# Sample attention as one straight pipeline of eight samples, and the causal mask of the recurrent heads put ahead of the gate scaling

## The chip, the core and the metric

One core of a Trainium2 chip runs the whole kernel. The metric is the time of one execution in microseconds (us) of device time. PE is TensorE, ACT ScalarE, DVE VectorE, POOL GpSimd, SP the engine that only issues transfers; a name with q (SPq, ACTq) is the instruction queue of that engine. All numbers are float32; a float32 matmul shows as two passes in the trace, a transpose as one.

## What is computed

One hybrid layer over a prompt of 512 tokens and 8 samples of 8 new tokens each. The parts that the change touches are the recurrent heads (the decay weights `exp(logd - m)` under a causal mask, and the normed, gated output) and the attention of each sample over 4096 cached positions. Cut to that:

```python
def mlstm_chunk(carry, inp):                     # 4 heads of 256
    logd = jnp.where(causal, b[..., :, None] - b[..., None, :] + li[..., None, :], -jnp.inf)
    s = jnp.einsum('bhtd,bhsd->bhts', q, k) * jnp.exp(logd - m_t[..., None])
    num = jnp.einsum('bhts,bhsv->bhtv', s, v) + a[..., None] * jnp.einsum('bhtd,bhdv->bhtv', q, C)
...
    h = h * jax.nn.sigmoid(o_pre)...
    h = rms_norm(h, norm_w).reshape(B, T, M_WIDTH)
    out = (h * jax.nn.silu(z.astype(jnp.float32))).astype(u.dtype)

def compress(rows, pe, w1, w2, k_norm):          # one vector per 16 positions, two layers
    hid = per[:, :-1, 0] + per[:, 1:, 1] + bias[:, None, :]
    out = jnp.einsum('bncgh,chd->bncgd', jax.nn.silu(hid), w2)
    return rms_norm(out[:, :, 0], k_norm), out[:, :, 1]

def nsa_sample(...):                             # for each of the 8 samples
    past = cache_kv[layer, page_table, :, 0:2]...          # 32 pages of 128 positions
    kc, vc = compress(...)
    o_cmp, idx = nsa_compressed(qq, tq, kc_b, vc_b, c_end, n_slc)   # top 16 of 65 blocks
    # o_sel: attention over the chosen blocks; o_win: over the last 512 positions
    o = gg[:, 0] * o_cmp + gg[:, 1] * o_sel + gg[:, 2] * o_win
    a_out = a_out * jax.nn.silu(az)
```

## The kernel before

The program runs stages one behind the other, each a block in which every engine has its own instruction list, in the order in which it is written, with semaphores between them: `project_in`, `mlstm_heads`, `compress_prompt`, `attend_prompt`, `attend_samples`, `combine_samples`, `project_out`. Nothing reorders an engine's list: an instruction that waits holds up all that stands behind it on its engine. At a block's end all engines meet.

**Recurrent heads.** For head h PE makes the scores of four 128-row tiles and of the samples (`scores`, L726 and L729) into two buffers `m_st`; ACT makes the decay weights `m_weights` (L846); POOL masks them (`causal`, L922), DVE multiplies scores and weights (L999) and so frees the score buffer for PE. POOL also scales the output gates by the norm weight (`norm_gate`, L915), for which it waits on transfers (the last is `landing<-m_norm_w`, issued by SP when the outputs of the head before are done). On POOL `norm_gate(h)` stands ahead of `causal(h)` for heads 1 to 3. DVE's `outputs(h)` waits for `norm_gate(h)`.

**Samples.** `attend_samples` sets up buffers and calls `sample_turn` nine times: once with compression alone (sample 0), six times in a hardware loop over b, and twice more. Each call is a block of its own with its own semaphores. A turn of the loop attends for sample b and compresses sample b+1:

- *pages.* A sample has 32 pages. Of each page one half (256 KB, `wide<-pages`, the buffer `comp`) feeds the compression and the other (256 KB, `s_kv<-pages`) the scores and values of the chosen blocks. `load_pages` looks up the page numbers of 8 pages in `ptab` (one register load each, L1457) and then issues the 8 transfers (L1460). SP loads three quarters of `s_kv` and all of `comp`; ACT loads the last quarter of `s_kv`, 8 pages, at the start of a turn.
- *compression.* PE: `hidden(i)`, four groups of 8 steps (L1529, one step is 128 weights by 512 columns) into two buffers `s_pH`; ACT splits each group out (L1648, L1649); POOL adds the two halves (L1808), ACT makes the sigmoid in three activations (L1654 to L1656), POOL multiplies (L1811); PE `second_layer` (L1541), ACT copies (L1665, L1668), POOL squares, sums and scales the keys (L1816 to L1826), PE turns them (L1550), ACT copies them to `s_kcT` (L1678).
- *attention.* Scores of the compressed keys (L1562) and the window (L1568), softmax by DVE and ACT, the turned probabilities and values, the choice of blocks on DVE (L1747 to L1757); then nine parts of scores over the cache (L1604, eight of 512 columns), which DVE masks (L1769) and of which it takes the maximum (L1776); ACT exponentials (L1714); and nine times: turn (L1619), copy on DVE (L1789), multiply with the values (L1629: all 128 query rows by 256 value columns, of which each row needs 64).
- the three results of a sample go to `o_scratch` in memory; `combine_samples` loads them all, applies the gates, adds and turns them and stores them for `project_out`.

Of the kernel before, what the change touches and what calls it, by code (L numbers as in the profile page):

```python
# [7 lines left out]
F32 = mybir.dt.float32  # L8
# [6 lines left out]
P = 128  # L15
# [547 lines left out]
def mlstm_heads(nc, B, a, o):  # L563
# [5 lines left out]
    with Semaphores(nc) as sem, ExitStack() as ctx:  # L569
# [329 lines left out]
        def _(pool):  # L899
# [502 lines left out]
def attend_samples(nc, B, a, o):  # L1402


    with ExitStack() as ctx:
        sb = lambda n, s, d=F32: ctx.enter_context(nc.sbuf_tensor(n, s, d))
        ps = lambda n, s: ctx.enter_context(nc.psum_tensor(n, s, F32))
        S = B.sample = Buffers()
        S.comp, S.kvp = B.comp, sb("s_kv", [P, NPG, CH])
        S.wnd = sb("s_wnd", [P, 2 * 2 * WIN])  # L1410
        S.cw1 = sb("cw1_sample", [P, 2, 8, P])
        S.scores = sb("s_scores", [P, PAST + TSA])
        S.first, S.second = sb("s_first", [P, KV * PAST // SEG]), sb("s_second", [P, KV * PAST // SEG])
        S.hidg = sb("s_hidg", [P, KV, NCMP_S + 1])
        S.kcn, S.kcms = sb("s_kcn", [P, 2, KV * AD]), sb("s_kcms", [P, 2 * KV])
        S.kcT, S.vc = sb("s_kcT", [P, 2, 256]), sb("s_vc", [P, 2, KV * AD])
        S.probT = sb("s_probT", [P, 2, 4, P])
        S.qb, S.nm = sb("s_qb", [P, 2, 64]), sb("s_newmask", [P, TSA])
        S.pgp, S.imp, S.top = sb("s_pgp", [32, 264]), sb("s_imp", [32, 72]), sb("s_top", [32, 2, 8])
        S.bias = sb("s_bias", [P, NBLK])  # L1420
        S.mx, S.rs, S.col = sb("s_mx", [P, 16]), sb("s_rs", [P, 16]), sb("s_col", [P, 8])
        S.rows = sb("s_rows", [P, 3, AD])
        S.pS, S.pT, S.pO, S.pH = (ps(n, [P, 2, CH]) for n in ("s_pS", "s_pT", "s_pO", "s_pH"))
        with Semaphores(nc) as sem, nc.Block() as block:
            loaded, zero = sem("s_loaded"), sem("s_zero")

            @block.sync
            def _(sp):
                sp.dma_start(S.cw1[:], a["cmp_w1"]).then_inc(loaded, 16)
                sp.wait_ge(loaded, 16)  # L1430

                sp.wait_ge(B.comp0_in, 16 * NPG)

            @block.vector
            def _(dve):
                nc.vector.memset(S.imp[:], 0.0)

                nc.vector.memset(S.kcn[:], 0.0)
# [7 lines left out]
        with nc.Fori(0, NB - 2) as b:  # L1446
            sample_turn(nc, B, a, b, attend=True, compress=True, load=True)
# [791 lines left out]
```

## Time and profile before

| | us |
|---|---|
| median of 3 runs | 2437.31 (2436.68 to 2440.33) |
| the profiled execution | 2436.53 |
| its span | 2434.8 |
| first hidden step of sample 0 to first transfer of `project_out`, in the trace | 1227.5 to 1954.0 |

The page of the profile gives busy time by engine, the span in 40 slices, the chain that ended last and the costliest groups. Busy time of PE counts the modelled length of each pass, so a stage can show PE at 90% and still lose time; a table of windows (busy time, granted clock and transfer share in stretches that one chooses) and the instructions in order of time show where.

### The profile page before, as it was taken

To read this page: it belongs to the slowest core of one execution; us is meant where nothing else is said; L and a number is where in the kernel's file an instruction comes from. 1 tells how busy PE (TensorE), PEld (TensorE's weight loads), DVE (VectorE), ACT (ScalarE), POOL (GpSimd) and SP (SyncE) were. 2 spreads that over 40 slices of the span, in tenths; PEclk is the share of its full clock that TensorE was granted. 3 is DMA by queue.
4 is the path that set the end of the run, shared out by engine and by line. 5 is a ranking of instruction groups with operands and counts; after the bars stand their busy time and mean duration, and the time that the engine had idled before them with its cause. 6 is when DMAs were issued, how large, how long until landed. Compare 5 with 4: busy or idle time off the path is not lost. (4 is left out here: it accounts for less than half of the span.)

```text
span 2434.8 us, 34702 instructions
## 1 busy us (share of the span) xinstructions
PE 2143.9 (88%) x12851; PEld 1740.2 (71%) x12851; DVE 851.7 (35%) x1644; ACT 697.7 (29%) x1337; POOL 154.1 (6%) x192
## 2 busy tenths in 40 slices
PE   7999999999988887799857889888986569999998
PEld 7999999999985555655533554455444369999998
DVE  6233255233323334456502233223323432233232
ACT  6332223333323222156511222122212031133221
POOL 0000000000001000000011121012111001010000
PEclk9999999999998887599978889988997779999999
DMA  5542333333313333111136657665753272222330
GB/s 188 172 152 75 93 98 112 98 107 98 113 65 125 129 132 121 47 53 57 61 125 233 218 191 241 226 226 186 240 198 114 63 283 94 70 90 76 98 103 25
DMA packets 167331, 316.19 MB, mean 130 GB/s; under 512 B 22365, under 2 KB 71902, under 8 KB 164130
## 3 DMA queue, kind: packets, MB, share of 16 engines
q1 hardware_dynamic: 156536, 297.33, 36.9%
q10 hardware_dynamic: 10666, 17.05, 2.1%
q8 instruction: 91, 1.49, 0.3%
q14 instruction: 38, 0.31, 0.0%
HBM read 281.53 MB, written 41.05 MB: 132 GB/s over the span
## 5 line engine op out<-in xcount | busy, mean ns | idle before, releaser
L250 PE MATMUL mm<-x_hi,w_hi 128*128 128x288 f32 x1696 | 369.1, 299 | 14.3 <-DVE w_lo L381 14.3
L250 PE MATMUL mm<-x_lo,w_hi 128*128 128x288 f32 x1696 | 364.1, 296 | 0.0
L250 PE MATMUL mm<-x_hi,w_lo 128*128 128x288 f32 x1696 | 364.1, 296 | 0.0
L250 PEld LDWEIGHTS mm<-x_hi,w_hi 128*128 128x128 f32 x1696 | 274.8, 190 | 15.9 <-issue 12.2
L250 PEld LDWEIGHTS mm<-x_lo,w_hi 128*128 128x128 f32 x1696 | 274.5, 190 | 0.0
L250 PEld LDWEIGHTS mm<-x_hi,w_lo 128*128 128x128 f32 x1696 | 274.2, 189 | 0.0
L381 DVE TENSOR_TENSOR w_lo<-w_raw,w_hi 128x1024 fp32r<-128x1024 f32 x106 | 129.8, 1225 | 386.4 <-ACT w_hi L280 386.4
L1529 PE MATMUL s_pH<-wide,cw_sample 128*128 128x512 f32 x512 | 239.4, 624 | 9.7 <-PEq L86 9.7
L1970 PE MATMUL o_mm<-o_feat_hi,o_w_hi 128*128 128x288 f32 x1024 | 225.7, 302 | 24.5 <-DVE o_feat_lo L2045 17.7
L1970 PE MATMUL o_mm<-o_feat_lo,o_w_hi 128*128 128x288 f32 x1024 | 222.0, 299 | 0.0
L1970 PE MATMUL o_mm<-o_feat_hi,o_w_lo 128*128 128x288 f32 x1024 | 221.6, 299 | 0.0
L280 ACT ACTIVATE w_hi<-w_raw 128x1024 fp32r<-128x1024 f32 x106 | 112.1, 1058 | 344.4 <-PE mm L250 344.4
L1529 PEld LDWEIGHTS s_pH<-wide,cw_sample 128*128 128x128 f32 x512 | 100.2, 201 | 130.1 <-issue 128.8
L1970 PEld LDWEIGHTS o_mm<-o_feat_hi,o_w_hi 128*128 128x128 f32 x1024 | 168.7, 192 | 26.9 <-issue 22.8
L1970 PEld LDWEIGHTS o_mm<-o_feat_lo,o_w_hi 128*128 128x128 f32 x1024 | 167.6, 192 | 0.0
L1970 PEld LDWEIGHTS o_mm<-o_feat_hi,o_w_lo 128*128 128x128 f32 x1024 | 167.5, 191 | 0.0
L1629 PE MATMUL s_pO<-s_kv,s_probT 128*128 128x256 f32 x512 | 134.2, 410 | 0.5 <-DVE s_probT L1789 0.5
L1629 PEld LDWEIGHTS s_pO<-s_kv,s_probT 128*128 128x128 f32 x512 | 100.8, 208 | 16.9 <-DVE s_probT L1789 3.1
L2039 DVE TENSOR_TENSOR o_w_lo<-o_w_raw,o_w_hi 128x2048 fp32r<-128x2048 f32 x32 | 73.4, 2293 | 111.4 <-ACT o_w_hi L2000 111.4
L1789 DVE COPY s_probT<-s_pT 128x512 f32<-128x512 f32 x64 | 44.1, 691 | 119.7 <-PE s_pT L1619 119.7
L1604 PE MATMUL s_pS<-s_kv,s_qb 128*64 128x512 f32 x256 | 68.9, 632 | 16.4 <-DMA s_kv<-pages 8.5
L2000 ACT ACTIVATE o_w_hi<-o_w_raw 128x2048 fp32r<-128x2048 f32 x32 | 60.8, 1900 | 49.2 <-DMA o_w_raw<-w_out 49.2
(395 smaller groups left out, 2487.6 us busy)
## 6 DMA issues: line engine op xcount, KB each, us to landing
wide<-pages SPq DMA_DIRECT2D x256, 256.0 KB, 4.1
w_raw<-w_in SPq DMA_DIRECT2D x106, 512.0 KB, 4.0
s_kv<-pages SPq DMA_DIRECT2D x192, 256.0 KB, 4.9
s_kv<-pages ACTq DMA_DIRECT2D x64, 256.0 KB, 7.3
o_w_raw<-w_out SPq DMA_DIRECT2D x16, 1024.0 KB, 7.8
o_w_raw<-ple_gate SPq DMA_DIRECT2D x16, 1024.0 KB, 6.7
m_state<-state SPq DMA_DIRECT2D x4, 2056.0 KB, 11.9
state_sample<-m_state SPq DMA_DIRECT2D x4, 2056.0 KB, 6.7
```

What stands on the lines that cost most here:

```text
L250: last = nc.tensor.matmul(mm[:, s % 3, y, 0:HALF], w[:, m % RING, kk, :], f[:, k, y * HALF:(y + 1) * HALF], start=k == 0 and i == 0, stop= ...
L280: s_.activation(whi[:, m % RING], raw[:, m % RING], ACT.Copy).then_inc(whi_done, 1)
L381: v.tensor_tensor(wlo[:, m % RING], raw[:, m % RING], whi[:, m % RING].bitcast(F32), ALU.subtract).then_inc(wlo_done, 1)
L1529: last = mm(S.pH[:, c, :], S.cw1[:, c, k, :], S.comp[:, 16 * cc:16 * cc + 16, k * 64 + c * 32:k * 64 + c * 32 + 32], start=k == 0, stop=k ...
L1604: last = mm(S.pS[64 * gp:64 * gp + 64, j % 2, :], S.qb[:, gp, :], S.kvp[:, 4 * j:4 * j + 4, gp * P:(gp + 1) * P], start=True, stop=True)
L1629: last = mm(S.pO[:, 0, 0:256], S.probT[:, q % 2, i, :], S.kvp[:, 4 * q + i, 256:512], start=q == 0 and i == 0, stop=False)
L1789: last = v.tensor_copy(S.probT[:, j % 2], S.pT[:, j % 2, :].rearrange("p (n r) -> p n r", r=P))
L1970: last = nc.tensor.matmul(mm[:, j % 2, x, 0:HALF], w[:, j % 2, k, :], f[:, k, cols], start=k == 0 and i == 0, stop=k == KD - 1 and i == 2)
L2000: s_.activation(whi[:, j % 2], raw[:, c % 2, :, (j % 2) * P:(j % 2 + 1) * P], ACT.Copy).then_inc(whi_done, 1)
L2039: v.tensor_tensor(wlo[:, j % 2], raw[:, (j // 2) % 2, :, (j % 2) * P:(j % 2 + 1) * P], whi[:, j % 2].bitcast(F32), ALU.subtract).then_inc( ...
```

## The change

**Heads.** POOL runs `causal(h)` ahead of `norm_gate(h)` for heads 1 to 3.

**Samples.** One function, one block, no loop and no `combine_samples`. All eight samples stand written out one behind the other on each engine, with semaphores that count on. The work of a sample stays the same in kind, with these differences:

- SP loads the window, all of `comp` and quarters 0 and 2 of `s_kv`; ACT loads quarters 1 and 3. The page numbers of a whole call (8 or 16) are looked up first, then the transfers are issued.
- `second_layer` (8 matmuls of 128 columns by a block-diagonal `s_cw2`, in place of 16 of 64 columns) and `keys_turned` of sample b moved from the end of the turn before to this turn's start, between the hidden groups of sample b+1.
- The values matmuls are done for two halves of the query rows, each with its own 128 value columns (64 weights by 128 columns, side by side in the array).
- DVE masks and takes the maximum in one instruction (`tensor_tensor_reduce`), and does the compression's sums and products that POOL did. POOL has nothing left in a turn.
- The gates are applied when a result is read out; three matmuls (`gather`) put a sample's output in place, and one transfer stores all at the end.

```diff
             for h in range(1, MH):
                 sample_u(h)
+                causal(h)
                 norm_gate(h)
-                causal(h)
...
+def load_pages(eng, ptab, pages, dst, part, first, begin, end, sem):
+    numbers = [eng.value_load(ptab[0:1, first + i:first + i + 1], min_val=0, max_val=pages.shape[0] - 1) for i in range(begin, end)]
+    for i, page in zip(range(begin, end), numbers):
+        eng.dma_start(dst[:, i, :], pages[bass.ds(page, 1), :, part * CH:(part + 1) * CH].rearrange("x p c -> p (x c)")).then_inc(sem, 16)
...
+            sp.dma_start(cw1[:], a["cmp_w1"]).then_inc(cw1_in, 16)
+            sp.dma_start(wnd[:], a["win_pages"][0]).then_inc(wnd_in, 16)
+            load_kv(sp, 0, 0)
...
+            sp.wait_ge(h_done, 2)
+            load_comp(sp, 1, 0, HP)
+            load_kv(sp, 0, 2)
+            sp.wait_ge(h_done, 4)
+            load_comp(sp, 1, HP, NPG)
+            for b in range(NB):
+                if b + 2 < NB:
+                    sp.wait_ge(h_done, 4 * (b + 1) + 2)
+                    load_comp(sp, b + 2, 0, HP)
+                if b + 1 < NB:
+                    sp.wait_ge(wo_done, b + 1)
+                    sp.dma_start(wnd[:], a["win_pages"][b + 1]).then_inc(wnd_in, 16)
+                if b + 2 < NB:
+                    sp.wait_ge(h_done, 4 * (b + 1) + 4)
+                    load_comp(sp, b + 2, HP, HP + QP)
+                if b + 1 < NB:
+                    sp.wait_ge(pv_done, PARTS * b + 2)
+                    load_kv(sp, b + 1, 0)
+                if b + 2 < NB:
+                    load_comp(sp, b + 2, HP + QP, NPG)
+                if b + 1 < NB:
+                    sp.wait_ge(pv_done, PARTS * b + 6)
+                    load_kv(sp, b + 1, 2)
...
+            for b in range(NB):
+                c = b + 1
+                window_scores(b)
+                hidden(c, 0, range(8))
+                if b:
+                    gather(b - 1)
+                second_layer(b)
+                hidden(c, 1, range(8))
+                keys_turned(b)
+                hidden(c, 2, range(0, 2))
+                compressed_scores(b)
+                hidden(c, 2, range(2, 5))
+                compressed_turned(b)
+                hidden(c, 2, range(5, 7))
+                compressed_values(b)
+                window_turned(b)
+                hidden(c, 2, range(7, 8))
+                hidden(c, 3, range(0, 2))
+                window_values(b)
+                block_bias(b)
+                for j in range(PARTS):
+                    scores(b, j)
+                    if j in (2, 4, 6):
+                        hidden(c, 3, range(1 + j // 2, 2 + j // 2))
+                hidden(c, 3, range(5, 8))
+                for j in range(PARTS + 1):
+                    if j < PARTS:
+                        turned(b, j)
+                    if j >= 1:
+                        values(b, j - 1)
...
+                act.wait_ge(wm_ready, b + 1)
+                s_.activation(pw[:, 0:WIN], pS[:, 1, :], ACT.Exp, bias=mx[:, 13:14], accum_out=rs[:, 13:14])
...
+                if b:
+                    act.wait_ge(pv_done, PARTS * b)
+                    load_kv(act, b, 3)
+                split(c, 0)
+                act.wait_ge(kv_done, b + 1)
...
+                act.wait_ge(mx_ready, b + 1)
+                for j in range(PARTS):
+                    if j == 2:
+                        split(c, 3)
+                    if j in (4, 5, 6):
+                        sigmoid(c, j - 4)
+                    s_.activation(chunk(j), chunk(j), ACT.Exp, bias=mx[:, 11:12], accum_out=rs[:, j:j + 1]).then_inc(p_ready, 1)
+                if c < NB:
+                    act.wait_ge(pv_done, PARTS * b + 4)
+                    load_kv(act, c, 1)
```

How the order moved, at the three places that the prediction speaks of. On ACT, from the last exponentials of a sample (L1714 before, L1742 after) to the copy of the next keys. Before, with the block's end behind the last row:

```order
L1714 ACTIVATE s_scores,s_rs<-s_scores,s_mx 128x512 x8
L1714 ACTIVATE s_scores,s_rs<-s_scores,s_mx 128x64
L1665 ACTIVATE s_vc<-s_pH 128x256
L1665 ACTIVATE s_vc<-s_pH 127x256
L1668 ACTIVATE s_kcn<-s_pH 128x256
L1668 ACTIVATE s_kcn<-s_pH 127x256
```

After, with the rows of 8 pages standing once where "..." is (a lookup, L1890, and a transfer, L1892, each eight times):

```order
L1742 ACTIVATE s_scores,s_rs<-s_scores,s_mx 128x64
L1890 TENSOR_LOAD ptab
...
L1892 DMA s_kv<-pages 128x512
L1704 ACTIVATE s_scores,s_rs<-s_pS,s_mx 128x512
L1705 ACTIVATE s_scores,s_rs<-s_pO,s_mx 128x64
L1890 TENSOR_LOAD ptab
...
L1892 DMA s_kv<-pages 128x512
L1680 ACTIVATE s_first<-s_pH 64x512
L1681 ACTIVATE s_second<-s_pH 64x512
L1716 ACTIVATE s_kcn<-s_pT 128x256
```

Two bursts of eight page loads now stand between a sample's last exponential and the copy of the next sample's keys; before, one burst stood at a turn's start and the copies followed the exponentials directly.

On PE, from the last values of a sample to the turned keys of the next. Before, across the block's end (the branch):

```order
L1631 MATMUL s_pO<-vsel_new,s_probT 128x256
L1550 MATMUL s_pH<-ident,s_kcn 128x128
L1550 MATMUL s_pH<-ident,s_kcn 128x127
L1550 MATMUL s_pH<-ident,s_kcn 128x128
L1550 MATMUL s_pH<-ident,s_kcn 128x127
L1478 UNCONDITIONAL_BRANCH
```

After:

```order
L1618 MATMUL s_pO<-vsel_new,s_probT 64x128 x2
L1532 MATMUL s_pS<-s_wnd,qblk 64x512 x2
L1534 MATMUL s_pO<-kwin_new,qblk 64x64 x2
L1504 MATMUL s_pH<-wide,cw_sample 128x512 x8
L1625 MATMUL s_pO<-s_pick,s_out 128x64 x3
L1515 MATMUL s_pT<-s_cw,s_hidg 128x128 x4
L1515 MATMUL s_pT<-s_cw,s_hidg 127x128 x4
L1504 MATMUL s_pH<-wide,cw_sample 128x512 x8
L1523 MATMUL s_pS<-ident,s_kcn 128x128
```

There is no branch, and two hidden groups (L1504) stand between the values and the turned keys (L1523), which wait for ACT and DVE.

On POOL, in the recurrent heads (the copy L908 brings in a head's sample inputs):

```order
 L908 COPY m_us<-upad 128x64 x2
+L922 AFFINE_SELECT m_weights<-m_weights 128x128 x4
 L915 TENSOR_TENSOR m_sgz<-m_sgz,landing 128x256 x4
 L915 TENSOR_TENSOR m_sgz<-m_sgz,landing 64x256
+L908 COPY m_us<-upad 128x64 x2
 L922 AFFINE_SELECT m_weights<-m_weights 128x128 x4
```

The four masks now come before the five multiplications that wait for transfers.

## Rows read from the trace of the kernel before

**Rows 1.** The page: busy time and its share of the span.
```profile
PE 2143.9 (88%) x12851; PEld 1740.2 (71%) x12851; DVE 851.7 (35%) x1644; ACT 697.7 (29%) x1337; POOL 154.1 (6%) x192
```

**Rows 2.** Windows: stretch, length, busy time by engine, clock, transfer share, GB/s.
```profile
1227.40:1290.20 62.80, 36.90 (x100) 19.58 (x100) 0.00 (x0) 10.29 (x18) 13.01 (x12) 0.74 0.39 134
1290.20:1864.70 574.50, 493.21 (x1904) 280.55 (x1904) 177.13 (x462) 135.79 (x329) 91.36 (x84) 0.92 0.61 204
1864.70:1931.80 67.10, 42.41 (x172) 26.12 (x172) 25.65 (x66) 9.11 (x29) 0.00 (x0) 0.76 0.41 142
1931.80:1954.00 22.20, 1.11 (x8) 0.93 (x8) 6.68 (x7) 0.00 (x0) 0.00 (x0) 0.56 0.30 63
```

**Rows 3.** Order of time at a turn's start: start, us, engine, line, what, idle before.
```profile
1455.52 1.12 PE L1562 MATMUL s_pS<-s_kcT,s_qb 128*64 128x255 f32 x4 [6.61 <-ACT s_qb L1688]
```

**Rows 4.** Recurrent heads: scores of head 1 (two rows) and head 3, and DVE's wait.
```profile
814.47 4.97 PE L726 MATMUL m_st<-m_qh,m_kh 128*128 128x512 f32 x8
825.06 2.93 PE L726 MATMUL m_st<-m_qh,m_kh 128*128 128x256 f32 x8 [5.63 <-DVE m_weights L999]
...
933.74 6.40 PE L726 MATMUL m_st<-m_qh,m_kh 128*128 128x512 f32 x16
...
DVE m_weights L999 <- POOL m_weights L922: 38.2, 2, 19.2
```

**Rows 5.** Order of time, PE at full clock; x counts passes.
```profile
1101.48 2.38 PE L1273 MATMUL a_pO<-a_pT,landing 128*64 128x512 f32 x16
1103.79 1.13 PE L1242 MATMUL a_pS<-ksel,landing 64*128 64x512 f32 x4
...
1311.24 7.03 PE L1529 MATMUL s_pH<-wide,cw_sample 128*128 128x512 f32 x16
...
1441.35 0.60 PE L1619 MATMUL s_pT<-ident,s_scores 128*128 128x128 f32 x4
1441.79 1.89 PE L1629 MATMUL s_pO<-s_kv,s_probT 128*128 128x256 f32 x8
...
1886.13 1.94 PE L1604 MATMUL s_pS<-s_kv,s_qb 128*64 128x512 f32 x8
```

**Rows 6.** Page loads: order of time, ACT's group, and SP's shortest, median, longest issue (ns).
```profile
1199.91 0.34 SPq L1223 DMA_DIRECT2D cat_scratch<-a_cat  x1
1202.91 2.11 SPq L1220 DMA_DIRECT2D wide<-pages  x4
...
1295.57 4.63 ACTq L1460 DMA_DIRECT2D s_kv<-pages  x8
...
L1692 ACT ACTIVATE s_scores<-s_pS,s_mx 128x255 f32<-128x255 f32 x8 | 3.8, 472 | 79.4 <-issue 79.4
...
L1460 SPq DMA_DIRECT2D s_kv<-pages x192: 332/333/1441, 1296.0 to 1893.2; - x192
```

**Rows 7.** Groups of the samples' stage: busy us, mean ns of one, idle before.
```profile
L1714 ACT ACTIVATE s_scores<-s_scores,s_mx 128x512 f32<-128x512 f32 x64 | 45.2, 708 | 61.2 <-DVE s_mx L1778 61.2
L1776 DVE TENSOR_REDUCE s_mx<-s_scores 128x1 f32<-128x512 f32 x64 | 43.9, 686 | 2.2
L1769 DVE TENSOR_TENSOR s_scores<-s_pS,s_bias 128x512 f32<-128x512 f32 x64 | 43.7, 683 | 56.4 <-PE s_pS L1604 56.4
L1648 ACT ACTIVATE s_first<-s_pH 64x512 f32<-64x512 f32 x32 | 18.8, 587 | 132.7 <-PE s_pH L1529 132.5
L1655 ACT ACTIVATE s_second<-s_second 128x1020 f32<-128x1020 f32 x8 | 8.4, 1054 | 0.3
```

**Rows 8.** PE behind two gaps (order of time), and a window behind the first.
```profile
1423.92 1.94 PE L1619 MATMUL s_pT<-ident,s_scores 128*128 128x128 f32 x8 [3.41 <-DVE s_rows L1782]
...
1890.50 1.94 PE L1604 MATMUL s_pS<-s_kv,s_qb 128*64 128x512 f32 x8 [2.43 <-DMA s_kv<-pages]
...
1424.00:1428.00 4.00, 4.00 (x13) 3.31 (x14) 1.38 (x2) 4.00 (x13) 0.00 (x0) 0.50 0.75 277
```

**Rows 9.** Order of time, last turn: ACT's exponential of the compressed scores.
```profile
1875.33 0.47 ACT L1692 ACTIVATE s_scores<-s_pS,s_mx 128x255 f32<-128x255 f32 x1 [10.28 <-issue]
```

More of the change, by code:

```diff
@@ L1452, in load_pages @@
-def load_pages(sp, ptab, pages, dst, part, first, begin, end, sem):
-    AHEAD = 8
-    assert begin % AHEAD == 0 and end % AHEAD == 0
-    with sp.Fori(begin // AHEAD, end // AHEAD) as i:
-        numbers = [sp.value_load(ptab[0:1, bass.ds(first + i * AHEAD + j, 1)], min_val=0, max_val=pages.shape[0] - 1)
-                   for j in range(AHEAD)]
-        for j, page in enumerate(numbers):
-            sp.dma_start(dst[:, bass.ds(i * AHEAD + j, 1), :].rearrange("p x c -> p (x c)"),
-                         pages[bass.ds(page, 1), :, part * CH:(part + 1) * CH].rearrange("x p c -> p (x c)")).then_inc(sem, 16)
@@ L1628, in _, with values @@
+            def values(b, q):
+                pe.wait_ge(t_copied, PARTS * b + q + 1)
+                if q == 0:
+                    pe.wait_ge(x_ready, 3 * b + 1)
+                for i in range(4 if q < NQ else 1):
+                    for gp in range(2):
                         if q < NQ:
[L1629 to L1631 removed]
@@ new lines, in values, with gather @@
+                last.then_inc(pv_done, 1)
+            def gather(b):
+                pe.wait_ge(x_ready, 3 * b + 3)
+                for y in range(3):
+                    last = mm(pO[:, 0, 256:320], out[:, y, :], pick[:], start=y == 0, stop=y == 2)
+                last.then_inc(xa_done, 1)
+            pe.wait_ge(gate_parts, 1)
+            pe.wait_ge(mine_ready, 1)
+            for y in range(3):
+                last = mm(pO[:, 0, y * NB:(y + 1) * NB], spreadg[:, y, :], mine[:], start=True, stop=True)
@@ L1638, in _ @@
+            gather(NB - 1)
         @block.scalar
@@ new lines, in split, with sigmoid @@
+                act.wait_ge(h_done, 4 * c + i + 1)
+                s_.activation(first[half(x), cc * CH:(cc + 1) * CH], pH[0:64, x, :], ACT.Copy)
+                s_.activation(second[half(x), cc * CH:(cc + 1) * CH], pH[64:128, x, :], ACT.Copy).then_inc(h_split, 1)
+            def sigmoid(c, part):
+                if c >= NB:
+                    return
+                if part == 0:
+                    act.wait_ge(hid_sum, c + 1)
+                    step(s_.activation(gate, first[:, 0:NH], ACT.Exp, scale=-1.0))
+                elif part == 1:
+                    step(s_.activation(gate, gate, ACT.Ln, bias=1.0))
+                else:
+                    s_.activation(gate, gate, ACT.Exp, scale=-1.0).then_inc(sig_ready, 1)
```

683 lines of the change are left out of this document (308 added, 375 removed).

## The prediction, made blind

> **What bounds the kernel now.** The page first: PE is busy 88% of the span [rows 1], so a stage matters where PE waits or does work that it could do faster. The windows show how far the samples' stage is from that: 726.5 us from sample 0's first hidden step to the first transfer of the last stage, in four parts: 62.8 us of compression alone, 574.5 us for seven turns (82.1 us each), 67.1 us for the last, 22.2 us for the combining [rows 2]. In the seven turns PE shows busy 493 us, clock 0.92; in the other parts half or less. What a turn loses at its seam is seen in order of time: PE's first work of a turn, at 1455.52, has 6.61 us of idle time before it, and it starts slowly [rows 3]. In the heads the order of time shows PE stopped 5.63 us on scores that DVE has not freed, and DVE 19 us on POOL's mask, twice [rows 4].
>
> **PE work of a new turn.** Prices at full clock [rows 5]: a hidden step is 7.03 less a tail over 8, 0.86 us, and a 512-column pass 0.43, so 0.835 ns a column. A transpose of 128 columns is 0.11. L1604 shows that two halves of 64 weights run side by side: four pairs of passes of 512 columns in 1.94 us, not eight times 0.43. So the values, until now 4 x 0.43 = 1.71 us a part, take half, 0.86. The second layer was 32 passes of 64 columns, and is 16 of 128 at 0.107: 1.7. A turn then: hidden 32 x 0.86 = 27.4; cache scores 7.1; turns 3.5; values 7.1; window scores 1.3; gather 0.65; second layer 1.7; the small ones (turned keys 0.43, compressed scores 0.43, turns and fold 0.64, values 0.43, window turns 0.53, window values 1.07, bias 0.1) 3.6. Sum 52.4 us against 82.1.
>
> What the half-width form adds: L1273 (1280 columns for each half, two passes: 2.14 us of columns) is followed by the next start 2.31 us after its own, so a change between full and half width costs about 0.17 us [rows 5]. A turn has some 36 such changes now, 18 of them in the values loop; 15 stand between turned keys and last score: 2.5 us. The Trainium skill, "TensorEngine Tiling (Array Packing)", Key Properties, speaks against this edit: changing the tiling mode drains the engine. The trace agrees, at 0.17 us; with a free change the turn below would be 2.5 us shorter.
>
> **What the turn waits for.** PE's list is not the limit: ACT is. Between a sample's last exponential and the copy of the next keys stand two bursts of eight pages. A page costs its issuer a lookup and an issue: four lookups took 1202.91 - 1200.25 = 2.66, so 0.67 each; ACT's eight issues took 4.63, 0.6 each; ACT's own wait for one burst is 79.4 / 8 = 9.9 us [rows 6]. Writing the addresses out doesn't cut this, since the 0.67 is from a load that was written out already. The chain from last exponential to turned keys (K): 9.9, window exponentials 1.1, 9.9, split 2 x 0.59 = 1.2, key copies 0.8 (half of a 512-column copy each, estimate), square and sum on DVE 1.5 (two of 0.69), logarithm and exponential 0.6, scaling 0.8: 25.7 us [rows 7]. PE meanwhile ends its values some 4.7 us after that exponential and has window scores, hidden 0, gather, second layer, hidden 1, 17.9 us with changes: ready at 22.6. It idles 3.1 us.
>
> From K to the last exponential: ten hidden steps and the small work 12.2; cache scores with three hidden steps between 9.7; changes 2.5; DVE's last part and maximum 0.7; then ACT: exponentials 8 x 0.71 + 0.5 = 6.2, split 1.2, three sigmoid steps 3.3, and 2.3 of waiting for the last hidden group and for DVE's sum of it [rows 7]. That is 38.1. A gap decides about the clock: after 3.41 us idle PE ran at 0.50, after 2.43 us at full speed [rows 8]. 3.1 lies between; I take the slow start, 4.3 us of work at half clock, +2.1, because it is nearer to 3.41. Turn: 25.7 + 38.1 + 2.1 = 65.9 us.
>
> DVE's merged mask-and-maximum has no row. Bounds: 0.68, what the mask alone takes, and 1.37, both as now [rows 7]. I take 0.7, as its operands are those of the mask: it is then faster than PE's 0.86 a part and hidden. At 1.37 the nine parts are DVE's pace, +2.7 us a turn. POOL's compression work (13.0 us in each turn's window) moves to DVE in 5 instructions, some 4.5 us, inside DVE's idle time save the 1.5 + 0.8 counted.
>
> **SP.** 48 pages a turn x 1.25 = 60 us and the window 0.4, in 65.9. It stands waiting for the fourth hidden group before its third call, so it is within 5 us of the limit; the last quarters of the compression pages land some 4 us before PE wants them. Transfers: 64 x 0.262 + 1.05 = 17.8 MB a turn; 204 GB/s at a share of 0.61 [rows 2] means 334 at full share, 53 us. Enough, not plenty.
>
> **First turn.** Hidden groups of sample 0 end at 1256.4 (0.6 us earlier, one block less). Sample 1's second 16 compression pages are SP's last of 40 from about 1243 (half of sample 0's hidden work): 40 x 1.25 = 50, 1293, landing 1298. K is 1297.5, the last exponential 1297.5 + 40.2 = 1337.7.
>
> **Six turns** of 65.9: 1733.
>
> **Last turn.** No hidden work: chain 24.5 to K (no split), 1757.6. From there to the exponential of the compressed scores: turned keys, copy, scores and maximum with PE at half clock, 3.6 by the same prices. Before it was 10.8 us from that exponential (1875.33) to the first cache scores (1886.13) [rows 5, 9], and the list between is the same: 10.8. Then cache scores at 0.86 a part with DVE's end 8.3, first exponential 0.8, nine turns and values 9 x (0.43 + 0.86 + 2 x 0.17) + 0.4 = 15.1, output (read-out, gather, product) 2.0: 1798.2. The final store is as before, 3.4 to the last stage's transfer: 1801.6, where before the last stage's first transfer stood at 1954.0. Gain 152.4, to be compared with 726.5 of the whole stage.
>
> **Heads.** Scores of head 1 go from 814.47 to 827.99, 13.5 us; those of head 3, whose masks were in time, take 6.4 [rows 4]. Head 2 has head 1's pattern. With the mask first both become like head 3: 7.1 x 2 = 14.2. The scaling is late then; DVE wants it for the outputs, 9 us or more after it is done, so it costs nothing; were it late, it would cost what it is late.
>
> **Sum.** 2436.5 - 152.4 - 14.2 = 2269.9 for the profiled execution, which is 0.8 under the median: 2270.7.
>
> **Rivals.**
> 1. ACT's bursts are hidden or cheaper (a page 1.0 us, or exponentials done earlier). Then PE's list closes the loop: 17.9 + 38.1 + 4.7 = 60.7, and SP's 60.4 stands right behind. Eight chains each 5 us shorter: 2236. For: three loops lie within 6 us. Against: both bursts have a row.
> 2. The load side or DVE is slower: merged instruction 1.37 (+22 over eight turns, 2294); or a page 1.5 us on SP when both queues issue, 72.4 us a turn, +6.5 x 7, 2317. For: issues of up to 1.44 us were seen [rows 6].
> 3. The pipeline doesn't do what it says: samples still run one chain after another and only the seam goes, 6.6 and its slow restart 2.1, seven times 61 us, plus heads: 2361. Against: the hidden groups now stand where PE waited.
> 4. Slower than before: page issue in place of compute. If each issue is held as the longest was, 1.44, a page costs 2.1 and SP's 48 pages 101 us a turn: 7 x 35 = 245 more, 2517. It decides from 65.9 + 166/7 = 89.6 us a turn, 1.86 us a page. Against: the median issue is 0.33.
>
> **Chances.** Forecast (turn of 63 to 69 us) 0.5; rival 1 0.2; rival 2 0.2; rival 3 0.05; rival 4 0.03; no change by some mishap of several of these 0.02. The range takes a 58 us turn (7 x 8 off, 2215, rival 1 with free width changes) to rival 2's second case with a little: 2212 to 2325, leaving out rivals 3, 4 and part of 2. A measurement here tells 0.2% from no change. Faster 0.95, same 0.02, slower 0.03.
>
> **What would show it.** Turns 65.9 us apart in order of time; ACT with two waits of 9.9 us marked issue each turn; PE idle about 3 us ahead of the turned keys at a clock of 0.50 after it; values parts of 0.86; merged DVE instruction near 0.7; DVE's 19 us waits in the heads gone, head 1's scores in 6.4 us. Wrong if PE waits for pages ahead of hidden groups (rival 2, 4), if the merged instruction is over 0.9, or if ACT's bursts end before PE is through the second hidden group (rival 1).

## The result, and the profile after

| | before | after |
|---|---|---|
| median, us | 2437.86 (2436.68 to 2440.33) | 2278.41 (2277.27 to 2284.42) |
| ratio, 95% interval | | 0.935 (0.9332 to 0.9368) |
| span of the profiled execution | 2434.8 | 2276.6 |

The forecast was 2270.7 us in a range of 2212 to 2325. The change gave 159 us where 167 were forecast. Set beside the terms of the sum, read from the two traces:

| term, us | forecast | measured |
|---|---|---|
| sample 0's first hidden step comes earlier (the heads) | 14.2 | 1227.5 - 1212.2 = 15.3 |
| from there to the first sample's last exponential | 110.2 | 1322.0 - 1212.2 = 109.8 |
| six turns | 6 x 65.9 = 395.4 | 1732.3 - 1322.0 = 410.3, or 6 x 68.4 |
| from the last turn's start to the last stage's first transfer | 68.5 | 1797.5 - 1732.3 = 65.2 |
| the last stage itself | 0 | 1.7 shorter |

The miss is the steady turn: 2.5 us too long, six times, 14.9 us. The other four terms are each within 4 us, all shorten the kernel against the forecast, and give 6.5 us of it back. The page's first line, which answers to [rows 1], shows PE's share of busy time up from 88% to 91% while it is busy 80 us less, and POOL down from 154 us to 51; the windows below show that none of it is left in the stage:

```profile
PE 2064.0 (91%) x13409; PEld 1661.7 (73%) x13409; DVE 830.1 (36%) x1639; ACT 697.3 (31%) x1328; POOL 50.7 (2%) x99
```

The samples' stage of after in windows, as in [rows 2]: compression of sample 0 up to the first turned keys, the first turn, five steady turns, the turn that runs into the last sample, and the end:

```profile
1212.20:1271.50 59.30, 49.56 (x120) 22.33 (x121) 6.82 (x14) 11.87 (x23) 0.00 (x0) 0.87 0.75 251
1271.50:1343.70 72.20, 61.08 (x343) 31.12 (x342) 23.13 (x64) 19.33 (x46) 0.00 (x0) 0.93 0.67 236
1343.70:1685.60 341.90, 303.83 (x1712) 155.42 (x1711) 115.72 (x320) 96.66 (x230) 0.00 (x0) 0.95 0.74 262
1685.60:1751.30 65.70, 46.94 (x311) 24.92 (x309) 22.64 (x62) 18.14 (x44) 0.00 (x0) 0.89 0.51 181
1751.30:1797.50 46.20, 35.81 (x254) 20.52 (x254) 17.15 (x54) 8.53 (x25) 0.00 (x0) 0.72 0.11 37
```

Five turns take 341.9 us, 68.4 each, and PE is busy 60.8 of that. Where it is not, the order of time shows (columns as in [rows 3]). The first row is the second hidden group, the next the turned keys, which the forecast expected PE to wait for; there is no wait at them. The wait is one row further down, for pages, and the four passes behind it take 3.78 us in place of 1.9:

```profile
1542.46 7.03 PE L1504 MATMUL s_pH<-wide,cw_sample 128*128 128x512 f32 x16
1549.33 0.61 PE L1523 MATMUL s_pS<-ident,s_kcn 128*128 128x128 f32 x4
1554.59 3.78 PE L1504 MATMUL s_pH<-wide,cw_sample 128*128 128x512 f32 x4 [4.65 <-DMA wide<-pages]
```

PE's waits from 1340 to 1752 us, summed by what ended them (us, times, longest); the keys' single wait is the last turn's:

```profile
PE s_pH L1504 <- DMA wide<-pages: 32.8, 6, 6.3
PE s_pS L1523 <- DVE s_kcn L1818: 10.9, 1, 10.9
PE s_pT L1602 <- ACT s_scores L1742: 7.6, 6, 1.3
```

SP, who issues those pages, in order of time. It waits for the fourth hidden group, which ends at 1516.28, then looks up and issues eight compression pages, eight pages of the scores' quarter 0, and the last eight compression pages (`wide` at 1539.83 to 1543.78), which are the ones that PE's third group still lacks:

```profile
1502.23 0.34 SPq L1473 DMA_DIRECT2D s_wnd<-win_pages  x1
1521.33 3.97 SPq L1892 DMA_DIRECT2D wide<-pages  x8
1529.93 5.30 SPq L1892 DMA_DIRECT2D s_kv<-pages  x8
1539.83 3.95 SPq L1892 DMA_DIRECT2D wide<-pages  x8
```

So the loop that closes a turn is: fourth group done (1516.28), 27.5 us of SP's work, 10.8 us until the last page has landed (1554.6), and 29.0 us from the third group's start to the fourth's end (1487.32 to 1516.28 in this turn). Together they are 67.3 us, which is how far apart the third group starts in two turns (1487.32 and 1554.59). The 10.8 are not the flight of a lone transfer. Issue to landing, for the first burst of eight and for the third (the windows 1521 to 1526 and 1539.5 to 1544.5; `wide` pages):

```profile
DMA to landing us min/median/max: 2.6/4.1/5.4
...
DMA to landing us min/median/max: 5.8/8.9/11.1
```

and the transfer engines in the two stretches from 1529.93 on, when ACT's sixteen pages come beside SP's (the last two numbers are the transfer share and GB/s):

```profile
1516.28:1529.93 13.65, 11.92 (x146) 9.29 (x144) 7.69 (x10) 9.02 (x19) 0.00 (x0) 1.00 0.47 155
1529.93:1539.83 9.90, 9.59 (x47) 4.78 (x46) 2.74 (x12) 1.07 (x4) 0.00 (x0) 1.00 0.95 333
1539.83:1554.60 14.77, 10.12 (x44) 5.82 (x42) 2.68 (x7) 4.77 (x11) 0.00 (x0) 0.91 1.04 382
```

The mean share of a turn is 0.74, which looks like room; these 25 us are full.

### The profile page after: what moved, and what is told of

It is laid out like the page before. It is cut to its first block and busy times, and to the rows that moved or that the text cites. A ratio compares the mean times of both kernels' runs of the same rounds, so it can differ in the third digit from the quotient of the medians.

```text
span 2276.6 us, 34604 instructions
## 1 busy us (share of the span) xinstructions
PE 2064.0 (91%) x13409; PEld 1661.7 (73%) x13409; DVE 830.1 (36%) x1639; ACT 697.3 (31%) x1328; POOL 50.7 (2%) x99
## 5 line engine op out<-in xcount | busy, mean ns | idle before, releaser
L1504 PE MATMUL s_pH<-wide,cw_sample 128*128 128x512 f32 x512 | 254.7, 640 | 54.1 <-DMA wide<-pages 51.5
L1504 PEld LDWEIGHTS s_pH<-wide,cw_sample 128*128 128x128 f32 x512 | 96.8, 201 | 176.1 <-issue 119.2
L1742 ACT ACTIVATE s_scores<-s_scores,s_mx 128x512 f32<-128x512 f32 (+1 forms) x72 | 48.3, 671 | 115.8 <-DVE s_mx L1857 115.1
L1615 PE MATMUL s_pO<-s_kv,s_probT 128*64 128x128 f32 x1024 | 70.9, 281 | 4.6 <-DVE s_probT L1863 4.6
L1329 ACT ACTIVATE a_p<-a_pS,a_nmax 128x128 f32<-128x128 f32 (+3 forms) x128 | 66.2, 524 | 16.8 <-DVE a_nmax L1368 16.8
L2016 ACT ACTIVATE o_w_hi<-o_w_raw 128x2048 fp32r<-128x2048 f32 x32 | 60.8, 1900 | 25.5 <-DMA o_w_raw<-w_out 25.5
L1615 PEld LDWEIGHTS s_pO<-s_kv,s_probT 128*64 128x64 f32 x1024 | 55.3, 138 | 16.1 <-issue 8.1
```

The source lines that it names most:

```text
L1329: s_.activation(prob[:, d % 2, g2, 0:(qt + 1) * P], pS[:, d % 2, g2, 0:(qt + 1) * P], ACT.Exp, bias=nmx[:, d, g2:g2 + 1], accum_out=rs[:, ...
L1504: last = mm(pH[:, x, :], cw1[:, x, k, :], comp[:, HP * cc:HP * cc + HP, k * 64 + x * 32:k * 64 + x * 32 + 32], start=k == 0, stop=k == 7)
L1615: last = mm(pO[half(gp), 0, 0:P], probT[:, q % 2, i, half(gp)], kvp[:, 4 * q + i, v0:v0 + P], start=q == 0 and i == 0, stop=False)
L1742: s_.activation(chunk(j), chunk(j), ACT.Exp, bias=mx[:, 11:12], accum_out=rs[:, j:j + 1]).then_inc(p_ready, 1)
L2016: s_.activation(whi[:, j % 2], raw[:, c % 2, :, (j % 2) * P:(j % 2 + 1) * P], ACT.Copy).then_inc(whi_done, 1)
```

## Experiments

"The changed kernel" is the kernel after, 2278.4 us. Each experiment's expectation was written before it ran.

**The heads alone.** The kernel before with one edit:

```diff
-                norm_gate(h)
                 causal(h)
+                norm_gate(h)
```

> The kernel before with the masks of heads 1 to 3 put ahead of the gate scaling, and nothing else. If the two halves of the change simply add, as the traces of before and after say (sample 0's first hidden step stands at 1227.5 before and at 1212.2 after), this gives 15.3 us of the gain: 2422.5 against 2437.9. Rival: the late scaling costs part of it elsewhere, or the start of the samples moved for another reason (one block less): below 12 us, 2426 or more.

Measured: 2420.9 (2419.5 to 2421.5) against 2438.2, ratio 0.993 (0.9909 to 0.995). Sample 0's first hidden step stands at 1211.8, 15.7 earlier. The gain of 17.2 us, in an interval of 12 to 22, fits the 15.3 that the trace gives this edit in the kernel after. The scores of the three heads there, which answer to [rows 4], all take what head 3's took before; DVE's waits for POOL's mask are gone:

```profile
814.81 6.35 PE L726 MATMUL m_st<-m_qh,m_kh 128*128 128x512 f32 x16
...
866.15 6.27 PE L726 MATMUL m_st<-m_qh,m_kh 128*128 128x512 f32 x16
...
917.07 6.40 PE L726 MATMUL m_st<-m_qh,m_kh 128*128 128x512 f32 x16
```

**Compression pages first.** The changed kernel with two of SP's bursts exchanged:

```diff
-                    load_comp(sp, b + 2, HP, HP + QP)
+                    load_comp(sp, b + 2, HP, NPG)
                 if b + 1 < NB:
                     sp.wait_ge(pv_done, PARTS * b + 2)
                     load_kv(sp, b + 1, 0)
-                if b + 2 < NB:
-                    load_comp(sp, b + 2, HP + QP, NPG)
```

> The changed kernel, with SP's list in another order: the last eight compression pages of a sample are issued directly behind the eight before them, and quarter 0 of the scores' pages after both. Theory A (the loop is closed by SP: third hidden group done, SP's three bursts, landing, third group's first step of the next sample): the 5.7 us wait of PE for pages and the slow clock behind it (1.9 us) go, a turn falls from 68.4 to 60.8 us, six turns give 45 us: about 2233. Theory B (the prediction's, ACT's two bursts close the loop at 65.9 us): 2.5 us a turn, 2263. Theory C (bytes are the limit, the pages land late whatever the order): no change, 2278.

Measured: 2232.6 (2227.8 to 2234.0), ratio to before 0.9152 (0.9131 to 0.9173); 45.8 us under the changed kernel. Turned keys now stand 60.75 us apart, and in order of time the work behind them starts at once:

```profile
1404.89 0.61 PE L1521 MATMUL s_pS<-ident,s_kcn 128*128 128x128 f32 x4
1405.34 1.88 PE L1502 MATMUL s_pH<-wide,cw_sample 128*128 128x512 f32 x4
```

The window of one such turn shows PE at full clock throughout:

```profile
1404.89:1465.64 60.75, 58.57 (x344) 30.50 (x343) 23.22 (x64) 19.33 (x46) 0.00 (x0) 1.00 0.82 293
```

The same bytes, the same issuers, one order changed: theory A holds, and theories B and C fall. What is left is PE's list, with the scaled keys ready 1.5 us before PE turns them. The turn is within 0.1 us of what rival 1 of the prediction gave for it (60.7; it had put the kernel at 2236).

**Page numbers looked up ahead of the wait.** To tell SP's time from the bytes of quarter 0, the order stays and only the eight lookups move:

```diff
+                    numbers = look(sp, b + 2, HP, HP + QP)
                     sp.wait_ge(h_done, 4 * (b + 1) + 4)
-                    load_comp(sp, b + 2, HP, HP + QP)
+                    issue(sp, numbers, comp, 0, HP, comp_in[1])
```

> The changed kernel with its order of transfers kept, but SP looks up the page numbers 16 to 23 before it waits for the fourth hidden group, so that they cost nothing behind it. Theory A (a serial chain on SP's issue time): the chain behind the fourth hidden group is 5.0 us shorter, PE's wait falls from 5.7 to 0.7 us and the slow clock behind it goes: 6.9 us a turn, six turns 41 us, 2237. Rival (comp_first won because it took quarter 0's bytes out of the way of the compression pages, not because of SP's time): the order is unchanged, so the pages land when they did, under 5 us of gain, 2274 or more.

Measured: 2234.4 (2228.6 to 2237.0). The waits for pages of the steady turns fall to between 0 and 1.0 us, and after them PE is at once at full speed (1.98 us for four passes):

```profile
1528.04 0.61 PE L1531 MATMUL s_pS<-ident,s_kcn 128*128 128x128 f32 x4
1529.66 1.98 PE L1512 MATMUL s_pH<-wide,cw_sample 128*128 128x512 f32 x4 [1.02 <-DMA wide<-pages]
```

The last eight compression pages still take 6.2 to 11.9 us to land; only their issue comes earlier. So five microseconds taken from SP's serial work give 44 us of the kernel, with the order of the bytes as it was.

**ACT's sixteen pages from POOL's queue.**

```diff
-            load_kv(act, 0, 1)
...
-            load_kv(act, 0, 3)
...
-                    load_kv(act, b, 3)
...
-                    load_kv(act, c, 1)
...
+            load_kv(pool, 0, 1)
+            load_kv(pool, 0, 3)
+            for b in range(NB - 1):
+                pool.wait_ge(pv_done, PARTS * b + 4)
+                load_kv(pool, b + 1, 1)
+                pool.wait_ge(pv_done, PARTS * (b + 1))
+                load_kv(pool, b + 1, 3)
```

> The changed kernel, with the two bursts of eight pages that ACT issues in a turn (quarters 1 and 3) issued by POOL, which has nothing else to do there. Theory A (SP's loop): the copies of the next keys come 7 to 14 us earlier, but PE still waits for the compression pages; 68.4 us a turn, 2278 within 5. Theory B (ACT's bursts close the loop): a turn falls to about 61 us, 2233. Rival D: transfers issued by POOL are slower or disturb the others, over 2290.

Measured: 2269.1 (2264.4 to 2273.7), 9 under the changed kernel and 4 below the band that theory A gave. The steady turns are not shorter: they are 69.3 us on average, where they were 68.4, and PE's wait for pages is 36.7 us over six, where it was 32.8. What went is ahead of the steady turns (first turned keys at 1268.2 in place of 1271.5) and in the last turn, which A had left out: PE waits 3.6 us for its keys there, not 10.9.

```profile
PE s_pH L1504 <- DMA wide<-pages: 36.7, 6, 6.7
...
PE s_pS L1523 <- DVE s_kcn L1813: 3.6, 1, 3.6
```

The prediction's reason for the turn's length, ACT's two bursts, is refuted for this kernel; so is the issuer as the cause of the late landing, since with POOL as issuer of the same transfers the pages come as late.

**Without those sixteen pages.**

```diff
-                    load_kv(act, b, 3)
...
-                    load_kv(act, c, 1)
...
-                    pe.wait_ge(kv_in[j // 2], 16 * QP * (b + 1))
+                    pe.wait_ge(kv_in[j // 2], 16 * QP * (1 if (j // 2) % 2 else b + 1))
```

> The changed kernel without ACT's sixteen page loads of a turn: quarters 1 and 3 of the scores' pages are loaded for sample 0 alone and used for all samples (so half of the selected attention's keys and values is computed from sample 0's pages). It takes away 16 of 64 page transfers a turn, which lie beside SP's last eight compression pages. In the changed kernel those eight need up to 11.1 us to land, at a transfer share of 1.04, where the eight issued at 1521 need 2.6 to 5.4. kv_pool kept the bytes and moved the issuer: no shorter turn. If the bunched bytes add to SP's chain, the landing falls by 4 to 6 us and PE's wait for pages to 0 to 1.5: a turn of 61 to 63 us, and 7.3 of the last turn's wait goes: 2278 - 6 x 6.5 - 7 - 3 = 2229, between 2222 and 2240. Rival: SP's issue time alone sets when the pages come: the turns stay at 68, only about 10 us go as in kv_pool: 2268.

Measured: 2226.5 (2224.1 to 2227.0). Turned keys stand 60.75 us apart, but for one turn of 61.7 with a page wait of 0.7 us. What this kernel computes is not the layer: it leaves out half of the scores' page loads of every sample but the first. Beside kv_pool this isolates the bytes: SP issues the same list in the same order in both, and here its last eight compression pages land in 2.7 to 5.6 us. Turned keys in order of time:

```profile
1464.81 0.61 PE L1523 MATMUL s_pS<-ident,s_kcn 128*128 128x128 f32 x4
1525.57 0.60 PE L1523 MATMUL s_pS<-ident,s_kcn 128*128 128x128 f32 x4
```

The window in which those pages fly, with a transfer share of 0.68:

```profile
1514.00:1528.00 14.00, 14.00 (x54) 7.58 (x54) 2.68 (x7) 4.78 (x11) 0.00 (x0) 1.00 0.68 223
```

So the loop had two parts that each could be cut alone: SP's serial 27.5 us, and 5 to 6 us of queueing among the transfers.

**Values at full width.** The changed kernel with the edit to the values taken back:

```diff
-                    for gp in range(2):
...
-                            last = mm(pO[half(gp), 0, 0:P], probT[:, q % 2, i, half(gp)], kvp[:, 4 * q + i, v0:v0 + P],
+                        last = mm(pO[:, 0, 0:256], probT[:, q % 2, i, :], kvp[:, 4 * q + i, 256:512],
...
-                scaled(2, 0, col[:, 1:2])
+                v.scalar_tensor_tensor(out[half(0), 2, :], pO[half(0), 0, 0:P], ...)
+                v.scalar_tensor_tensor(out[half(1), 2, :], pO[half(1), 0, P:2 * P], ...)
```

> The changed kernel, with the values matmuls at full width again (128 query rows by 256 value columns), so 4 x 0.43 = 1.71 us a part in place of 1.02: 6.2 us more work for PE a turn. Theory A (SP's loop): the work fills the wait for pages (5.7 us) and the slow clock behind it goes; a turn is then PE's list, 60.8 + 6.2 = 67.0 us, 1.4 less than now; the first and last turn pay in full, 12.4; six turns give 8.4 back: about 2282. Theory P (PE's list is what a turn lasts): 8 x 6.2 = 50 us more, 2328.

Measured: 2272.1 (2271.0 to 2273.4): more work for PE, and 6.3 us *faster*, where I had expected 3.7 slower (2282). Steady turns are 64.2 to 69.0 us, with waits for pages of 0 to 3.2. Theory A's mechanism is seen, its price was wrong: a part of turn and values takes 2.16 us at full width (1506.38 to the next 1508.54) and 1.61 at half (1518.69 to 1520.30), 0.55 apart where I had put 0.69 and the columns alone would give 0.86:

```profile
1506.38 1.89 PE L1613 MATMUL s_pO<-s_kv,s_probT 128*128 128x256 f32 x8
1508.11 0.60 PE L1602 MATMUL s_pT<-ident,s_scores 128*128 128x128 f32 x4
1508.54 1.89 PE L1613 MATMUL s_pO<-s_kv,s_probT 128*128 128x256 f32 x8
```

and, in the changed kernel:

```profile
1518.69 0.66 PE L1602 MATMUL s_pT<-ident,s_scores 128*128 128x128 f32 x4
1519.28 1.09 PE L1615 MATMUL s_pO<-s_kv,s_probT 128*64 128x128 f32 x16
1520.30 0.66 PE L1602 MATMUL s_pT<-ident,s_scores 128*128 128x128 f32 x4
```

The missing 0.86 - 0.55 = 0.31 us goes with two changes of width a part, 0.15 to 0.16 each, near the 0.17 that the prediction read from [rows 5]. The Trainium skill, "TensorEngine Tiling (Array Packing)", Key Properties, has such a change drain the engine; the trace agrees and gives it this size.

**Both: pages first, values at full width.** The two diffs above together.

> Both edits: the compression pages issued ahead of quarter 0, and the values matmuls at full width. The fourth corner beside the changed kernel (2278.4), comp_first (2232.6) and wide_values (2272.1). If the half-width values save PE time always, and only the late pages hid it, full width now costs what it costs in an undisturbed turn of wide_values, 64.2 against 60.75 us: seven turns and a last one, 8 x 3.5 = 28 us, 2261. Rival: the half-width form isn't faster in itself (its changes of width eat it): 2233 within 5.

Measured: 2257.5 (2257.2 to 2263.6). The steady turns are 64.11 us, without a wait for pages. The four corners:

| | values at half width | values at full width |
|---|---|---|
| pages late | 2278.4 | 2272.1 |
| pages first | 2232.6 | 2257.5 |

The half-width values are worth 24.9 us, and cost 6.3 in the kernel as it was changed. The edit is sound; its gain was turned into a wait, and the wait slowed the clock.

**Mask and maximum apart.**

```diff
-                        last = v.tensor_tensor_reduce(blocked(chunk(j)), blocked(pS[:, j % 2, :]), by, ...)
+                        v.tensor_tensor(blocked(chunk(j)), blocked(pS[:, j % 2, :]), by, ALU.add).then_inc(masked, 1)
+                        dve.wait_ge(masked, NQ * b + j + 1)
+                        last = v.tensor_reduce(mx[:, j:j + 1], chunk(j), AX, ALU.max)
```

> The changed kernel with mask and maximum as two DVE instructions again (0.68 and 0.69 us in place of one of 0.69). The prediction put this at 2.7 us a turn, 22 us in all. The trace has the fourth hidden group's first steps between the scores, and this group starts SP's chain, so what DVE adds to the scores lengthens the loop: PE's scores with their hidden steps take 11.1 us for nine parts now, DVE's nine would take 12 to 13: 1.5 us a turn by theory A, 12 us, 2290. Rival: it hides behind the wait for pages, 2278 within 3.

Measured: 2288.0 (2285.3 to 2289.3), 9.6 more than the changed kernel and within 2 us of what theory A gave. The groups of DVE, the merged form in the changed kernel first, then the two instructions here:

```profile
L1852 DVE CUSTOM_DVE_ANT_1 s_scores<-s_pS,s_bias 128x512 f32<-128x512 f32 x64 | 44.3, 691 | 46.4 <-PE s_pS L1589 46.0
```
```profile
L1853 DVE TENSOR_TENSOR s_scores<-s_pS,s_bias 128x512 f32<-128x512 f32 x64 | 44.0, 687 | 17.4 <-PE s_pS L1590 17.4
L1855 DVE TENSOR_REDUCE s_mx<-s_scores 128x1 f32<-128x512 f32 x64 | 43.9, 686 | 2.2
```

The merged instruction costs what the mask alone did, the lower bound that the prediction took (reading the maximum out adds 0.08 us). Apart, the two lengthen a turn by 1.2 us, under half of the 2.7 given for that end.

**ACT's chain made longer.** comp_first, with eight idle lookups ahead of each of ACT's bursts:

```diff
+            if eng is nc.scalar:
+                for i in range(QP):
+                    eng.value_load(B.ptab[0:1, b * NPG + q * QP + i:b * NPG + q * QP + i + 1], ...)
             load_pages(eng, B.ptab, a["pages"], kvp, 1, b * NPG, q * QP, (q + 1) * QP, kv_in[q])
```

> comp_first, with each of ACT's page bursts preceded by eight further lookups whose results are not used. A lookup costs 0.52 us in the trace, so each burst is 4.2 us longer, two 8.4 us a turn. In comp_first the scaled keys are ready 1.3 us before PE turns them. If ACT's chain stands that close behind PE's list, a turn grows by 8.4 - 1.3 = 7.1 us and 0 to 2 of slow clock: 60.75 to 68 or 70, six turns 43 to 55, the last turn 8.4: 2284 to 2296. Rival (ACT's bursts lie beside other work with room, so ACT is no loop worth a forecast): under 15 us, 2248.

Measured: 2286.9 (2285.7 to 2293.8), 54 us more than comp_first. Now PE does wait for the keys in every turn, and turns them at half speed (1.11 us in place of 0.61):

```profile
1416.50 1.11 PE L1524 MATMUL s_pS<-ident,s_kcn 128*128 128x128 f32 x4 [5.84 <-DVE s_kcn L1819]
1484.82 1.11 PE L1524 MATMUL s_pS<-ident,s_kcn 128*128 128x128 f32 x4 [5.93 <-DVE s_kcn L1819]
```

ACT's chain is real, as the prediction described it. But in comp_first it ends 1.5 us before PE is ready for the keys, where the prediction had it end 3.1 us after.

**Towards a better kernel.** Three further kernels build on comp_first. all_early lets POOL issue ACT's bursts, and in the first turn looks page numbers up before the waits and loads sample 1's compression pages ahead of quarter 2. split_by_use gives SP the compression pages and the window, POOL all pages of the scores, with each lookup ahead of its wait. split_by_use_late is that with POOL's quarters 2 and 3 of sample 0 held back:

```diff
+            for q in range(4):
+                if q == 2:
+                    pool.wait_ge(h_done, 4)
+                load_kv(pool, 0, q)
```

> comp_first, and POOL issues ACT's two bursts, and in the first turn SP looks up the page numbers of sample 1 before it waits and issues its 32 compression pages ahead of quarter 2 of sample 0. From 2232.6: the last turn's 10.5 us wait for the keys loses ACT's burst, 7.3 us; the first turn's two waits of PE for pages (9.7 and 8.1 us) go nearly whole, with their slow clock: about 21 us; the steady turns stay PE's list at 60.75 us. About 2204. Rival: transfers of POOL and SP at once make the first pages land later, and only half of the 21 us comes: 2215.

> SP issues the compression pages and the window alone, each sixteen looked up before the wait that frees their buffer; POOL issues all pages of the scores; ACT none. From all_early (2211.9, steady turns of 61.9 us with PE waiting 0.4 to 2.3 us for pages): the waits go and the turns fall to PE's list, 60.75 us, 7 us in all: 2205. Rival: the pages of both queues bunch and land late in places, as all_early's did: 2212 or more.

> split_by_use, with POOL waiting for the fourth hidden group of sample 0 before it loads quarters 2 and 3 of sample 0's pages. In split_by_use all seven steady turns were 60.75 us, but PE waited 12.0 us for sample 1's first compression pages, while POOL's four bursts were under way; all_early, with two bursts there, waited 1.6 us. If those bytes are what made them late, the keys of sample 0 are turned at 1260 in place of 1270 and the rest follows: 2219 - 10 = 2209, under all_early's 2212. Rival: the wait has another cause (the issue of SP itself), 2219.

Measured: all_early 2211.9 (2208.7 to 2213.9), ratio to before 0.9062 (0.9045 to 0.9079), the fastest of all; 8 over what I expected, between the two theories' figures: its first turn is as forecast, and the six turns from sample 0's turned keys on are 61.9 us on average, with waits for pages of 0.4 to 2.3. split_by_use 2219.3 (2214.4 to 2222.6), 14 over what I expected: every steady turn is 60.75 us, but POOL's 32 pages of sample 0 now fly beside sample 1's first compression pages, and PE waits 12.0 us for those. split_by_use_late 2221.1 (2217.4 to 2224.7): holding two quarters back moved the wait and did not remove it; my expectation missed by 12 us, since it looked at the first half of the pages alone. PE's waits in the first turn, split_by_use first, then split_by_use_late:

```profile
1251.61 9.96 PE L1497 MATMUL s_pH<-wide,cw_sample 128*128 128x512 f32 x16 [12.02 <-DMA wide<-pages]
```
```profile
1242.99 7.13 PE L1497 MATMUL s_pH<-wide,cw_sample 128*128 128x512 f32 x16 [0.64 <-DMA wide<-pages]
...
1271.65 3.78 PE L1497 MATMUL s_pH<-wide,cw_sample 128*128 128x512 f32 x4 [12.44 <-DMA wide<-pages]
```

The transfer share from 1226 to 1240 us, where those first pages fly, is 1.02 in split_by_use, and their landing takes up to 17.6 us. The share alone doesn't tell this: in all_early, with two bursts of POOL's in place of four, it is 1.05 in the same stretch, and the pages land in at most 8.1 us. A kernel with all_early's first turn and split_by_use's steady ones was not tried.

## Why the prediction was right, and where it was off

The number lies in the range, and the turn of 68.4 us in the forecast's case of 63 to 69, but in part by luck: by the prediction's own signs its mechanism was wrong. PE waits for pages ahead of a hidden group, and ACT's second burst ends at 1543.36, before PE is through the second hidden group at 1549.33. Another loop, not the one forecast, closes the turn at nearly the same length.

*What bounds the kernel.* Right: the samples' stage was PE's list with gaps at its seams, and it fell from 726.5 to 585.3 us. The runs price three edits in it or ahead of it: the heads 17 us, the merged instruction 9.6, the half-width values -6.3. The rest of the 159 us, some 139, is left for the single stream with its new order, the work moved from POOL to DVE and the folding in of `combine_samples` (22.2 us before [rows 2]); no run takes these apart.

*PE's list.* Right in sum: 52.4 us of work and 36 width changes at 0.17 are 58.5; an undisturbed turn is 60.75, with 1.3 us of it a wait for ACT's exponential.

*The chain over ACT.* The step that failed is "PE's list is not the limit: ACT is", by a mis-sized term. A burst was put at 9.9 us, from ACT's idle time in the turn of before [rows 6]; there the burst opened a block. In the new stream the two bursts take 7.1 and 7.5 us of ACT's time (ACT's rows, and as the last one DVE's scaling of the keys):

```profile
1527.26 0.33 ACT L1742 ACTIVATE s_scores<-s_scores,s_mx 128x64 f32<-128x64 f32 x1
...
1529.37 5.36 ACTq L1892 DMA_DIRECT2D s_kv<-pages  x8
1534.77 0.69 ACT L1704 ACTIVATE s_scores<-s_pS,s_mx 128x512 f32<-128x512 f32 x1 [7.09 <-DVE s_mx L1810]
...
1543.36 0.59 ACT L1680 ACTIVATE s_first<-s_pH 64x512 f32<-64x512 f32 x1 [7.52 <-issue]
...
1547.30 0.69 DVE L1818 TENSOR_TENSOR s_kcn<-s_kcn,s_kcms 128x512 f32<-128x512 f32 x1 [0.61 <-ACT s_kcms L1720]
```

A lookup was 0.52 us, not 0.67, and the first burst's lookups begin at 1525.0, while the exponentials run on to 1527.6:

```profile
L1890 ACTq TENSOR_LOAD <-ptab x5: 272/275/283, 1525.0 to 1527.1; - x5
```

From the last exponential to the scaled keys ACT's chain is 20.4 us (1527.59 to 1547.99), not 25.7: 5.2 of the difference are the two bursts. PE's own list needs 21.7 to get there (forecast 22.6), so it is PE that sets the time of the turned keys.

*SP.* The second step that failed: "the last quarters of the compression pages land some 4 us before PE wants them". They landed 4.7 to 6.3 us after PE had begun to wait for them. The issue time had been put too high, if anything (1.25 us a page; measured 54.7 us for 48 pages and the window, 1.13). Mis-sized was the landing: the prediction allowed 5 us where it wrote it out (1293 to 1298), and it is up to 11.1 us in the crowd. PE also came for the pages 4 us earlier, as its keys were not late. The prediction did weigh transfers, at 53 us of 65.9, "enough, not plenty"; a mean over the turn says nothing of 25 us in which both queues issue. The Trainium skill, "DMA: Bandwidth & Descriptors", Issuing engines are not separate DMA queues, says that transfers of all issuers share the engines and that a second issuer only saves the issuing time, "usually small relative to the DMA itself". On the first half kv_pool agrees: another issuer for the same bytes, and the pages as late. On the second the trace differs: a page of 256 KB costs SP 1.13 us, and at 382 GB/s its bytes need 0.69.

*The errors met.* In the turn shown it is 4.0 us less to the turned keys, and 6.9 more from them to the last exponential (1480.46 to 1527.59, 47.1 against 40.2). Of these the wait for pages is 6.25 us (5.5 on average over six turns). The slow restart was forecast at 2.1 us behind a wait for the keys; it came, 1.9 us, behind the wait for pages.

*The first turn.* 109.8 against 110.2, and here two errors cancel. The landing of sample 1's last pages was right: expected at 1298 on the clock of before, it came at 1281.1 + 15.3 = 1296.4. But the turned keys were put at 1297.5, without a working, and came at 1271.5 + 15.3 = 1286.8, although PE had waited 9.7 us for sample 1's first pages by then. From there to the last exponential it took 50.5 us, not 40.2, since PE waited 8.9 us for the last pages behind the turned keys.

*The last turn.* 3.3 us shorter than forecast: 5.5 less to the turned keys (19.0 for 24.5), as ACT's bursts are shorter, and 2.2 more behind them (46.2 for 44.0).

*The merged instruction, the heads, the half-width form.* 0.69 us for 0.7; 15.3 for 14.2; 0.15 to 0.16 for 0.17 a change of width.

*Rivals.* Rival 1 is the kernel one exchange of two bursts away (2232.6 for 2236; its own words, eight chains of 5 us, give 2231, and 2236 is seven of them). Rival 2 had the right side of the miss and the wrong reason, a slower issue. Rivals 3 and 4 did not show.

## What to carry to other kernels

When engines are put into one stream, work out every loop that a buffer makes, not only the one over the compute engines: buffer free, issuer's serial work, landing in the traffic of that moment, first use. An issuer's lookups belong ahead of its wait and the transfer that is wanted first at the head of its list; here that exchange was worth 46 us and no work was removed. A cut in the busiest engine's work says nothing until that loop is shorter than its list: the same edit was worth +25 us on one side of that point and -6 on the other.

## What the runs showed of the hardware

- Transfers of 256 KB land in 2.6 to 5.4 us after issue when the transfer share of the stretch is 0.47, and in up to 11.1 at 1.04; with POOL and SP at once in split_by_use, up to 17.6 at 1.02, but at most 8.1 in all_early at 1.05. Who issues the other transfers made no difference in kv_pool (6.8 to 10.8 us for the last eight pages, where it was 5.8 to 11.1); without them it was 2.7 to 5.6.
- Whether PE starts slowly behind a wait is worth 1.9 us in its next four passes. After the wait of 4.65 us for pages the granted clock was 0.50, 1.2 GHz (first line below); after one of 1.02 us four passes took 1.98 us, full speed. In between, wide_values has 3.18 us of idle time followed by 0.51 (second line) and 2.45 us followed by 0.50, while four passes behind 2.29 us in all_early took 1.98 us and PE ran at full speed behind 2.43 us before the change [rows 8]. What decides between such close cases the rows don't show.

```profile
1555.00:1558.00 3.00, 3.00 (x4) 0.76 (x3) 0.00 (x0) 0.00 (x0) 0.00 (x0) 0.50 1.04 385
```
```profile
1543.00:1546.00 3.00, 3.00 (x4) 1.08 (x4) 0.00 (x0) 0.00 (x0) 0.00 (x0) 0.51 1.05 386
```

- ACT's queue looks up page numbers while its last exponentials still run, 2.6 us ahead in the rows above. A burst behind compute work held ACT for 7.1 and 7.5 us, one at a block's start for 9.9 [rows 6].
